# Router stage and first expert: kept memory re-laid, last ring place loaded sooner, biases moved, expert 0 gathered as columns

## The chip, the cores and the metric

One core of one Trainium2 chip runs the whole layer in one launch. The metric is the device time in microseconds (us); lower is better.

## What is computed

One decoder layer over 256 tokens of width 1024, in float32: a projection, a convolution group and a gated linear attention group, the output projection added to x (the sum is called x2 here), then a mixture of experts and a final norm. What matters here is the mixture:

```python
logits = (xf @ w_router + b_router).astype(jnp.float32)      # xf = RMSNorm(x2)
top_v, top_i = lax.top_k(logits, TOP_K)                      # 4 of 32
gates = jax.nn.softmax(top_v, axis=-1)
...
gu = xb @ w_gate_up[eid] + b_gate_up[eid]
gate = jnp.minimum(gu[:, :D_FF], SWIGLU_LIMIT)
up = jnp.clip(gu[:, D_FF:], -SWIGLU_LIMIT, SWIGLU_LIMIT)
glu = gate * jax.nn.sigmoid(gate * SWIGLU_ALPHA)
return ((up + 1.0) * glu) @ w_down[eid] + b_down[eid]
```

The weights of all 32 experts (12.6 MB each, 403 MB in all) have to come from memory.

## The kernel before

**Tiling.** The 256 tokens are two tiles (t = 0, 1) of 128. K = 1024 is eight blocks of 128 (k = 0 to 7). An item is one expert with up to 64 of its tokens (SLOTS); items 0 to 31 are the 32 experts in order, and further ones exist only for experts with more than 64 tokens.

**The ring.** Expert weights are loaded in chunks of 2 MB (4096 float32 on each of 128 partitions) into a ring of 12 places. An item has 6 chunks: 0 to 3 are gate and up, 4 and 5 are down, so the ring holds two items. The chunks are numbered g = 0, 1, 2, ...; SyncE (SP) issues the loads in the order of the list in its block, L496, each behind a wait: g = 1 to 11 wait for the mixer's buffers that lie in the same places, g = 12 and later wait until TensorE has used the chunk 12 before. g = 12 goes in four quarters (0.5 MB), g = 13 to 17 in halves (1 MB), since item 0's chunks free piece by piece (semaphores s_quarter, s_half, s_used). From item 6 on the loads go in pairs of 4 MB. g = 11, the last place, waits for s_lg 2, both tiles' logits: its place (10) holds the columns of x2 (h_t), the scaled router weights (wr_g) and the partial logits until then.

**The router stage.** TensorE (PE) runs the output projection, turns x2 into columns (L1606, transposes), and multiplies by the router weights (L1622 in parts for tile 0, L1612 for tile 1). ScalarE (ACT) copies columns and takes squares. VectorE (DVE) then makes, for each tile, logits (L1162), their eight largest (L1164), and the mask of the four chosen experts (L1165 to L1167, "chosen"). PE multiplies the mask by a triangle of ones to rank the tokens (L1663, L1678), DVE makes of it a selection matrix p_row for expert 0 (L1171, L1173), and PE gathers the rows of x2 by it (gather, L1634: the selection is the stationary operand, 512 columns of x2 stream past). ACT copies the gathered rows to x_row (L759), PE turns them (turn_first, L1700), DVE scales them into x_t (L1234), and the first product of item 0 (gate_up, L1750) can start. idle (L1562) is a matmul whose result is not used. Softmax gates are made beside this (L1199 to L1205, L1229), turned (L1705), and used from item 0's end on.

**An item.** gate_up over chunks 0 to 3, turn_gates (L1795) between chunks 0 and 1, turns of the result (L1789), down over chunks 4 and 5 (L1770), the gather and turn of the next item (L1634, L1692), and a scatter (L1814).

**The biases.** ACT issues the loads of b_gate_up (bias_t) and b_down (bdn, four pieces) early in the mixer, L666 to L669.

## Time and profile before

| | us |
|---|---|
| median of 3 runs | 1028.8 |
| lowest and highest | 1027.85, 1029.49 |
| profiled execution, device time | 1027.81 |
| its span on the core | 1026.0 |

Outside the span lie 1.8 us of the profiled execution. The granted TensorE clock of the span was 0.998 of full speed. The page's second part cuts the span into 40 equal slices of 25.65 us, and for each shows the engines' busy share in tenths, the share of the 16 DMA engines and the rate in GB/s. "Windows" below are the same for stretches that were asked for. The chain of waits is the work that ended last, followed back from the end. Times in the timeline are from the start of the span.

### The profile page before, as it was taken

To read this page: it belongs to the slowest core of one execution; us is meant where nothing else is said; L and a number is where in the kernel's file an instruction comes from. 1 tells how busy PE (TensorE), PEld (TensorE's weight loads), DVE (VectorE), ACT (ScalarE), POOL (GpSimd) and SP (SyncE) were. 2 spreads that over 40 slices of the span, in tenths; PEclk is the share of its full clock that TensorE was granted. 3 is DMA by queue.
4 is the path that set the end of the run, shared out by engine and by line. 5 is a ranking of instruction groups with operands and counts; after the bars stand their busy time and mean duration, and the time that the engine had idled before them with its cause. 6 is when DMAs were issued, how large, how long until landed. Compare 5 with 4: busy or idle time off the path is not lost.

```text
span 1026.0 us, 12540 instructions
## 1 busy us (share of the span) xinstructions
PE 1000.9 (98%) x5004; PEld 411.9 (40%) x5004; DVE 273.3 (27%) x673; ACT 149.6 (15%) x299; POOL 9.7 (1%) x27
## 2 busy tenths in 40 slices
PE   9999999999999999999999999999999999999996
PEld 7799733333333333333333333333333333333333
DVE  2878322222212222222222212222121212122122
ACT  2311211111111111111111111111111111111112
POOL 1010000000000000000000000000000000000000
PEclk9999999999999999999999999999999999999999
DMA  9996799999999999999999999999999999999995
GB/s 381 395 376 253 304 393 428 427 426 434 429 429 431 429 431 431 432 433 436 432 429 432 429 431 431 432 433 436 432 429 431 431 429 432 427 429 428 425 420 237
DMA packets 24716, 423.97 MB, mean 413 GB/s; under 512 B 3048, under 2 KB 3696, under 8 KB 6384
## 3 DMA queue, kind: packets, MB, share of 16 engines
q1 hardware_dynamic: 23328, 420.78, 96.5%
q10 hardware_dynamic: 1360, 2.79, 0.7%
q8 instruction: 21, 0.34, 0.1%
q14 instruction: 7, 0.06, 0.0%
HBM read 422.51 MB, written 1.05 MB: 413 GB/s over the span
## 4 chain that ended last, share of the span: by engine, by line
PE 80%; DMA 18%; issue 1%; DVE 0%; ACT 0%; SPq 0%; POOL 0%; ACTq 0%; PEldq 0%; DVEq 0%; POOLq 0%
PE bank L1750 34%; PE bank L1770 19%; DMA ring<-in_w_expert 18%; PE bank L1416 5%; PE y L1814 5%; PE bank L1634 5%; PE bank L1789 3%; PE bank L1692 1%; PE bank L1466 1%; PE bank L1408 1%; PE y L1567 1%; PE bank L1599 1%; PE bank L1795 1%; PE bank L1872 1%; PE y L1856 0%
## 5 line engine op out<-in xcount | busy, mean ns | idle before, releaser
L1750 PE MATMUL bank<-ring,x_t 128*64 128x512 f32 x1984 | 447.1, 597 | 0.0
L1770 PE MATMUL bank<-ring,act 128*64 128x512 f32 x992 | 230.8, 596 | 11.7 <-DMA ring<-in_w_expert 11.7
L1750 PEld LDWEIGHTS bank<-ring,x_t 128*64 128x64 f32 x1984 | 133.9, 136 | 261.9 <-issue 258.1
L1272 DVE TENSOR_TENSOR gu_b<-bank,bias_t 128x512 f32<-128x512 f32 x64 | 44.3, 692 | 326.6 <-PE bank L1789 326.5
L1770 PEld LDWEIGHTS bank<-ring,act 128*64 128x64 f32 x992 | 68.3, 137 | 142.9 <-issue 140.0
L773 ACT COPY gu_sb<-bank 128x512 f32<-128x512 f32 x64 | 37.5, 587 | 222.7 <-PE bank L1750 222.7
L1225 DVE TENSOR_TENSOR x_t<-bank,cols 128x512 f32<-128x512 f32 x30 | 20.8, 692 | 165.1 <-PE bank L1692 165.1
L1814 PE MATMUL y<-z,p_t 64*128 64x512 f32 x248 | 61.6, 615 | 0.0
L1634 PE MATMUL bank<-x_sb,p_row 128*64 128x512 f32 x256 | 60.6, 593 | 0.0
L1211 DVE TENSOR_SCALAR p_row<-slot,rank,rstd 128x64 f32<-128x64 f32 x62 | 16.7, 312 | 164.5 <-PE bank L1795 164.5
L777 ACT ACTIVATE act<-gu_b 128x256 f32<-128x256 f32 x62 | 25.9, 418 | 191.7 <-DVE gu_b L1278 191.7
L1789 PEld LDWEIGHTS bank<-ident,gu_sb 128*128 128x128 f32 x256 | 26.8, 140 | 50.7 <-issue 50.2
L1789 PE MATMUL bank<-ident,gu_sb 128*128 128x128 f32 x256 | 42.0, 286 | 0.1
L769 ACT COPY p_t<-bank 128x256 f32<-128x256 f32 x31 | 11.6, 373 | 189.2 <-PE bank L1795 189.2
L1634 PEld LDWEIGHTS bank<-x_sb,p_row 128*64 128x64 f32 x256 | 18.2, 137 | 35.6 <-issue 35.4
L781 ACT COPY z<-bank 128x512 f32<-128x512 f32 x31 | 18.2, 587 | 90.7 <-PE bank L1770 90.7
L1814 PEld LDWEIGHTS y<-z,p_t 64*128 64x128 f32 x248 | 21.3, 186 | 20.0 <-issue 14.6
L1288 DVE TENSOR_TENSOR act<-act,gu_b 128x256 f32<-128x256 f32 x62 | 26.4, 425 | 6.5
L1283 DVE SCALAR_TENSOR_TENSOR gu_b<-gu_b 128x256 f32<-128x256 f32 x64 | 27.2, 424 | 2.2
L765 ACT COPY x_row<-bank 128x512 f32<-128x512 f32 x31 | 18.2, 587 | 63.0 <-PE bank L1634 63.0
L1692 PEld LDWEIGHTS bank<-ident,x_row 128*128 128x128 f32 x124 | 13.0, 140 | 31.2 <-issue 31.2
L1692 PE MATMUL bank<-ident,x_row 128*128 128x128 f32 x124 | 19.5, 280 | 4.8 <-PE bank L1770 4.8
(264 smaller groups left out, 515.2 us busy)
## 6 DMA issues: line engine op xcount, KB each, us to landing
ring<-in_w_expert SPq DMA_DIRECT2D x66, 4096.0 KB, 34.3
ring<-in_w_expert SPq DMA_DIRECT2D x48, 2048.0 KB, 16.9
ring<-in_w_expert SPq DMA_DIRECT2D x18, 1024.0 KB, 10.1
ring<-in_w_in SPq DMA_DIRECT2D x4, 2048.0 KB, 27.4
ring<-in_w_out SPq DMA_DIRECT2D x2, 2048.0 KB, 28.9
ring<-in_w_in SPq DMA_DIRECT2D x2, 1024.0 KB, 13.3
ring<-in_w_expert SPq DMA_DIRECT2D x4, 512.0 KB, 4.3
ring<-in_w_down_last SPq DMA_DIRECT2D x4, 512.0 KB, 28.4
```

The source lines that it names most:

```text
L773: act_e.copy(gu_sb[:, h, :], bank[h][:, :]).then_inc(s_guk, 1)
L777: act_e.activation(act_of(it)[:, 4 * h:4 * h + 4, :], gu_b[:, 0, :, :], ACT.Sigmoid, scale=ALPHA).then_inc(s_sig, 1)
L1272: dve.tensor_tensor(gu_b[:, :, :, :], bank[2][:, :].rearrange("p (f a s) -> p a f s", a=2, f=4), bias_t[:, :, 4 * h:4 * h + 4, ds(e, 1)] . ...
L1283: dve.scalar_tensor_tensor(out=gu_b[:, 1, :, :], in0=gu_b[:, 1, :, :], scalar=1.0, in1=gu_b[:, 0, :, :], op0=ALU.add, op1=ALU.mult).then_i ...
L1288: dve.tensor_tensor(act_of(it)[:, 4 * h:4 * h + 4, :], act_of(it)[:, 4 * h:4 * h + 4, :], gu_b[:, 1, :, :], ALU.mult).then_inc(s_av, 1)
L1416: ins = mm(acc[:, m, :], w[:, k, m * P:(m + 1) * P], h[:, k, :], start=first and m == 0 and k == 0, stop=last and k == 3, skip_group_check ...
L1634: ins = mm(bank[3][a * SLOTS:(a + 1) * SLOTS, :], p_row[:, t, :], xs[:, t, a * HALF:(a + 1) * HALF], start=t == 0, stop=t == TT - 1)
L1692: ins = nc.tensor.transpose(bank[3][:, f * P:(f + 1) * P], x_row[:, f * P:(f + 1) * P], ident[:, :])
L1750: ins = mm(bank[h][a * SLOTS:(a + 1) * SLOTS, :], x_t_of(it)[:, k, :], w[:, kk, a, :], start=k == 0, stop=k == KT - 1)
L1770: ins = mm(bank[0][a * SLOTS:(a + 1) * SLOTS, :], act_of(it)[:, k, :], w[:, kk, a, :], start=k == 0, stop=k == KT - 1)
L1789: ins = nc.tensor.transpose(bank[2][:, f * P:(f + 1) * P], gu_sb[:, h, f * P:(f + 1) * P], ident[:, :])
L1814: mm(y_ps[t][nn][:, :], p_t_of(it)[r, t * P:(t + 1) * P], z[r, :], start=first, stop=False, skip_group_check=True).then_inc(s_y, 1)
```

## The change

1. **Kept memory.** The columns of x2 go to a tile of their own, h2 (8 KB a partition), in memory that later holds act, gu_b, p_t, bdn and gates_t. wr_g, parts_sb and ident4, and three new small tiles, go to where bias_t will be. Place 10 of the ring is thereby free after the sixth product of the output projection.
2. **The last place.** g = 11 is issued ahead of g = 9 and waits for that product instead of both logits.
3. **The biases** are now loaded by SP, ahead of g = 12: bdn (one piece, laid out on the host) behind s_lg 2, bias_t behind s_p0 2. ACT's five issues are gone.
4. **Expert 0 ranked alone.** For tile 1, DVE compares the logit of expert 0 with the fourth largest (first_c, one element a partition) instead of first making the whole mask; PE ranks that column alone; DVE makes p_row for tile 1 straight from PSUM. The mask, the full rank and the gates come later, beside item 0.
5. **Gathered as columns.** gather_first has 128 x 128 blocks of x2 as stationary operand and p_row (64 columns) streaming, so the columns x_t come out directly: no copy to x_row, no turn. It comes in three parts (k 0 to 1, 2 to 3, 4 to 7), each scaled by DVE by itself (keep_first). Tile 0's part is spread over the waits where idle stood; of tile 1, k 4 to 7, the full rank and the counts stand inside item 0, between its second and third k, and the turn of the gates between chunk 1's halves.

```diff
+        h2 = at("h2", [P, TT, KT, P], 16384)
+        wr_g, parts_sb, ident4, slot0, first_c, first_r = row((
...
+            def load_biases():
+                sp.wait_ge(s_lg, 2)
+                sp.dma_start(bdn[:, :], b_down).then_inc(s_bdn, 16)
+                sp.wait_ge(s_p0, 2)
+                sp.dma_start(bias_t[:, :, :, :], ...).then_inc(s_bias, 16)
+            for g in [0, 1, 2, 6, 7, 3, 4, 5, 8, 11, 9, 10] + list(range(12, len(LOAD_ORDER))):
...
                     elif g == 11:
-                        sp.wait_ge(s_lg, 2)
+                        sp.wait_ge(s_prod, PRODUCTS * len(BLOCKED) + 6)
...
+            def choose_first():
+                dve.tensor_tensor(first_c[:, :], lg[:, 1, 0:1], lmax[:, 1, TOP - 1:TOP], ALU.is_ge).then_inc(s_first, 1)
+                dve.wait_ge(s_first, 1)
+                dve.tensor_tensor(first_r[:, :], first_c[:, :], rstd[:, 1:2], ALU.mult).then_inc(s_first, 1)
...
+            mark_chosen(1)
+            keep_first(0, 0, 2, s_xt_a)
+            keep_chosen(1)
+            keep_first(1, 2, 4, s_xt_a)
...
+            def gather_first(t, ks):
+                for k in ks:
+                    i = 0 if k < 2 else 1 if k < 4 else 2
+                    k0 = (0, 2, 4)[i]
+                    ins = mm(bank[FIRST_BANK[i]][:, (k - k0) * SLOTS:(k - k0 + 1) * SLOTS], xs[:, t, k * P:(k + 1) * P], p_row[:, t, :],
...
+                if known == 0:
+                    gate_up(it, 0, range(0, 2))
+                    gather_first(1, range(4, KT))
+                    rank_second()
+                    gate_up(it, 0, range(2, 4))
+                    gate_up(it, 1, range(0, 2))
+                    turn_all_gates()
+                    turn_gates(it)
+                    gate_up(it, 1, range(2, 4))
```

On PE, from the end of the logits of tile 1 to the second chunk of item 0. Before, in program order (the last field is the operand's size and count; x_row are gathered rows, x_t the columns of the item):

```order
L1612 MATMUL y<-wr_g,g_h 128x32
L1674 MATMUL y<-chosen,ones 128x32 [waits first_p_row_ready]
L1634 MATMUL bank<-x_sb,p_row 64x512 x2
L1678 MATMUL y<-chosen,before 128x32 [waits chosen_ready]
L1680 MATMUL y<-ones,chosen 32x1 x2
...
L1700 MATMUL bank<-ident,x_row 128x128 [waits first_x_row_half_ready]
...
L1750 MATMUL bank<-ring_49,x_t 64x512 [waits slot11_loaded,first_x_t_half_ready]
L1750 MATMUL bank<-ring_49,x_t 64x512 x3
L1750 MATMUL bank<-ring_49,x_t 64x512 [waits x_t_ready]
```

After:

```order
L1652 MATMUL y<-wr_g,h_62 128x32
L1675 MATMUL bank<-p_row,x_sb 128x64 x5
L1727 MATMUL y<-chosen,ones 128x1
L1730 MATMUL y<-first_c,before 128x1 [waits second_tile_of_first_expert_chosen]
L1602 MATMUL bank<-before,ones 128x128
L1675 MATMUL bank<-p_row,x_sb 128x64 [waits first_p_row_ready]
L1675 MATMUL bank<-p_row,x_sb 128x64 x3
L1801 MATMUL bank<-ring_49,x_t 64x512 [waits slot11_loaded,first_x_t_columns_ready]
L1801 MATMUL bank<-ring_49,x_t 64x512 x3
L1675 MATMUL bank<-p_row,x_sb 128x64 x4
L1739 MATMUL y<-chosen,ones 128x32 [waits chosen_ready]
L1740 MATMUL y<-chosen,before 128x32
```

The full mask's wait (chosen_ready) and four of the gathering matmuls have moved behind the first two k of item 0, and the turn of x_row is gone.

On SP, the loads before item 0's first chunk is given back (ring_54 is two places, of them place 10; 128x4096 is a whole chunk). Before:

```order
L484 DMA ring_53<-in_w_expert 128x4096 [waits quadrant_ready,y_gla_ready]
L484 DMA ring_53<-in_w_expert 128x4096 [waits block_product_ready]
L484 DMA ring_54<-in_w_expert 128x2048 [waits out_projected] x2
L484 DMA ring_54<-in_w_expert 128x4096 [waits logits_ready]
L484 DMA ring_49<-in_w_expert 128x1024 [waits first_chunk_quarter_used] x3
```

After:

```order
L494 DMA ring_54<-in_w_expert 128x4096 [waits block_product_ready]
L494 DMA ring_53<-in_w_expert 128x4096 [waits block_product_ready]
L494 DMA ring_54<-in_w_expert 128x2048 [waits out_projected] x2
L508 DMA bdn<-in_b_down 128x512 [waits logits_ready]
L510 DMA bias_t<-in_b_gate_up 128x512 [waits first_p_row_ready]
L494 DMA ring_49<-in_w_expert 128x1024 [waits first_chunk_quarter_used] x3
```

The whole chunk of place 10 has moved ahead of three loads, and two bias loads stand between the ring's last filling and its first refill.

## Rows read from the trace of the kernel before

**Rows 1.** The page: rate in 40 slices; busy time and share of PE.

```profile
GB/s 381 395 376 253 304 393 428 427 426 434 429 429 431 429 431 431 432 433 436 432 429 432 429 431 431 432 433 436 432 429 431 431 429 432 427 429 428 425 420 237
PE 1000.9 (98%) x5004; PEld 411.9 (40%) x5004; DVE 273.3 (27%) x673; ACT 149.6 (15%) x299; POOL 9.7 (1%) x27
```

**Rows 2.** Windows: stretch and length, busy us (count) by engine, clock, DMA share, GB/s.

```profile
85.00:95.00 10.00, 10.00 (x83) 9.74 (x82) 9.22 (x18) 1.12 (x3) 0.00 (x0) 1.00 0.14 32
115.00:125.00 10.00, 9.71 (x72) 8.11 (x73) 4.27 (x20) 2.80 (x11) 0.00 (x0) 1.00 0.45 151
130.00:135.00 5.00, 5.00 (x26) 1.57 (x24) 2.16 (x10) 0.56 (x2) 0.00 (x0) 1.00 0.89 329
200.00:700.00 500.00, 497.12 (x2330) 170.51 (x2328) 108.67 (x288) 64.45 (x127) 0.00 (x0) 1.00 1.00 431
```

**Rows 3.** Waits of PE over the span: us in total, times, longest.

```profile
PE bank L1770 <- DMA ring<-in_w_expert: 11.7, 8, 1.8
```

**Rows 4.** The chain of waits in order of time: start, us, what.

```profile
129.76 3.58 PE bank L1750 x16
133.71 5.30 PE bank L1750 x24
156.92 3.58 PE bank L1750 x16
967.29 38.46 DMA ring<-in_w_expert
```

**Rows 5.** SP's load line in narrow windows: one issue's time, us to its landing.

```profile
L484 SPq DMA_DIRECT2D ring<-in_w_expert x1: 328/328/328, 124.7 to 124.7; - x1
DMA to landing us min/median/max: 7.5/7.5/7.5
...
L484 SPq DMA_DIRECT2D ring<-in_w_expert x1: 328/328/328, 130.8 to 130.8; - x1
DMA to landing us min/median/max: 3.5/3.5/3.5
...
L484 SPq DMA_DIRECT2D ring<-in_w_expert x1: 328/328/328, 132.5 to 132.5; - x1
DMA to landing us min/median/max: 4.8/4.8/4.8
...
L484 SPq DMA_DIRECT2D ring<-in_w_expert x1: 327/327/327, 137.3 to 137.3; - x1
DMA to landing us min/median/max: 7.3/7.3/7.3
```

**Rows 6.** Timeline of PE: start, us, line, operation, count.

```profile
124.08 0.63 PE L1612 MATMUL y<-wr_g,g_h 128*128 128x32 f32 x4
124.54 0.39 PE L1674 MATMUL y<-chosen,ones 128*128 128x32 f32 x2
126.07 0.41 PE L1678 MATMUL y<-chosen,before 128*128 128x32 f32 x2
127.11 1.08 PE L1634 MATMUL bank<-x_sb,p_row 128*64 128x512 f32 x4
129.69 1.51 PE L1750 MATMUL bank<-ring,x_t 128*64 128x512 f32 x6
```

**Rows 7.** Timeline of DVE and ACT in the same stretch.

```profile
121.46 0.15 DVE L1187 TENSOR_SCALAR rest<-rest 128x1 f32<-128x1 f32 x1
125.10 0.20 DVE L1164 MAX8 lmax<-lg 128x8 f32<-128x32 f32 x1
126.51 0.19 DVE L1171 SCALAR_TENSOR_TENSOR rank<-y,chosen 128x32 f32<-128x32 f32 x1 [0.50 <-PE y L1678]
126.74 0.31 DVE L1173 TENSOR_SCALAR p_row<-slot,rank,rstd 128x64 f32<-128x64 f32 x1
128.24 0.65 ACT L759 COPY x_row<-bank 128x256 f32<-128x256 f32 x2 [0.70 <-PE bank L1634]
129.14 0.43 DVE L1234 TENSOR_TENSOR x_t<-bank,cols 128x256 f32<-128x256 f32 x1 [0.30 <-PE bank L1700]
```

More of the change, by code:

```diff
@@ L297, in build @@
         s_late = sem("router_weights_loaded")
[L298 removed]
+        s_bias = sem("gate_up_biases_loaded")
+        s_bdn = sem("down_biases_loaded")
         s_gfin = sem("g_final_loaded")
@@ L665, in _ @@
             act_e.dma_start(br_bc[:, :], b_router.partition_broadcast(P)[:, 0, :]).then_inc(s_late, 16)
-            act_e.dma_start(bias_t[:, :, :, :], b_gate_up.rearrange("p (a f e) -> p a f e", a=2, f=F // P)).then_inc(s_bias, 16)
-            for i in range(SPLITS):
-                c = slice(i % 2 * HALF, (i % 2 + 1) * HALF)
-                act_e.dma_start(bdn[i * E:(i + 1) * E, :], b_down[0][:, c]).then_inc(s_bias, 16)
             def keep_v(n):
@@ L754, in _ @@
             act_e.activation(ex[:, :, :], ex[:, :, :], ACT.Exp).then_inc(s_le, 1)
-            for f in range(2):
-                act_e.wait_ge(s_xg, 1)
-                act_e.copy(x_row[:, f * 256:(f + 1) * 256], bank[3][:, f * 256:(f + 1) * 256]).then_inc((s_xr_a, s_xr)[f], 1)
             act_e.preload_act_table_set("sigmoid_and_others")
             def keep_gathered(it):
-                act_e.wait_ge(s_xg, it + 1)
+                act_e.wait_ge(s_xg, it)
                 act_e.copy(x_row[:, :], bank[3][:, :]).then_inc(s_xr, 1)
@@ L1181, in _ @@
             dve.wait_ge(s_lg, 1)
-            choose(0)
+            raw_to_logits(0)
+            mark_chosen(0)
+            keep_chosen(0)
             dve.wait_ge(s_const, 3)
-            rank_and_place(0)
+            link(rank(0))
+            dve.tensor_scalar(p_row[:, 0, :], slot1[:, 0:SLOTS], rank1[:, 0, 0:1], rstd[:, 0:1],
+                              ALU.is_equal, ALU.mult).then_inc(s_p0, 1)
             dve.wait_ge(s_ss, TT + 3)
@@ L1561, in idle @@
                 for _ in range(n):
-                    mm(bank[1][:, 0:P], ones[:, :], before[:, :], start=True, stop=True)
+                    mm(bank[0][:, 0:P], ones[:, :], before[:, :], start=True, stop=True)
             def multiply_rows(acc, y, w, first, last):
@@ L1667, in _, with rank_second @@
             logits(1, 4, 6)
+            pe.wait_ge(s_p0, 1)
+            gather_first(0, range(0, 1))
             pe.wait_ge(s_x2, 3)
             transpose_x(1, 6, 8)
[L1670 removed]
+            gather_first(0, range(1, 3))
             pe.wait_ge(s_trD, 1)
             logits(1, 6, 8)
[L1673 to L1681 removed]
+            gather_first(0, range(3, KT))
+            mm(bank[5][:, 2 * E:2 * E + 1], ones[:, :], chosen[:, 0, 0:1], start=True, stop=False)
+            pe.wait_ge(s_first, 1)
+            mm(bank[5][:, 2 * E:2 * E + 1], before[:, :], first_c[:, :], start=False, stop=True).then_inc(s_rk0, 1)
             idle(1)
             pe.wait_ge(s_p0, 2)
[L1684 to L1685 removed]
+            gather_first(1, range(0, 4))
             nb = BLOCKS - 1
+            def rank_second():
+                pe.wait_ge(s_cho, 2)
+                mm(bank[5][:, E:2 * E], ones[:, :], chosen[:, 0, :], start=True, stop=False)
+                mm(bank[5][:, E:2 * E], before[:, :], chosen[:, 1, :], start=False, stop=True).then_inc(s_rk, 1)
+                for t in range(TT):
+                    ins = mm(bank[7][0:E, 256:257], chosen[:, t, :], ones[:, 0:1], start=t == 0, stop=t == TT - 1)
+                ins.then_inc(s_cnt, 1)
             def turn_gathered(it):
[L1690 removed]
+                pe.wait_ge(s_xr, it)
                 for f in range(4):
@@ L1693, in turn_gathered, with turn_all_gates @@
                 ins.then_inc(s_xT, 1)
-            def turn_first():
-                for i in range(2):
-                    pe.wait_ge((s_xr_a, s_xr)[i], 1)
-                    for f in range(2 * i, 2 * i + 2):
-                        ins = nc.tensor.transpose(bank[(2, 4)[i]][:, f % 2 * P:(f % 2 + 1) * P], x_row[:, f * P:(f + 1) * P], ident[:, :])
-                    ins.then_inc((s_xT_a, s_xT)[i], 1)
-                    idle(1 - i)
+            def turn_all_gates():
                 pe.wait_ge(s_gtk, 2)
```

127 lines of the change are left out of this document (70 added, 57 removed).

## Prediction

> **What bounds the kernel now.** First the page's rates and busy shares [rows 1]: PE is busy 98% of the span, yet from the seventh slice on the rate stands at 425 to 436 GB/s and does not move. The windows say the same: 431 GB/s at a DMA share of 1.00 over the 500 us from 200 to 700 [rows 2]. So two engines look full at once, and the question is which would finish first alone. The chain of waits answers it. Item 0 begins at 129.76 and item 1 at 156.92 [rows 4]: 27.2 us of PE work for an item. Its 12.6 MB at 431 GB/s take 29.2 us. PE therefore runs ahead by 2 us an item, gives ring places back sooner than they can be filled, and late in the kernel stands still for weights, eight times and 11.7 us in all [rows 3]; the last long stretch of the chain is 38.46 us of expert loads [rows 4]. From item 0 to the end the kernel is a queue of loads that never runs dry. A microsecond of PE work in the items is worth nothing; the time can fall only if this queue starts sooner.
>
> When does it start? The ring holds twelve chunks, and the thirteenth (g = 12) needs a quarter of item 0's first chunk given back. Its first quarter is issued at 130.8 and lands 3.5 us later [rows 5], against PE's start of item 0 at 129.69 [rows 6]: 1.12 us from start to issue. The last place, g = 11, is issued at 124.7 and lands after 7.5 us, at 132.2 [rows 5]. So before, the two conditions meet at nearly the same moment: the loads have just filled the ring when the first quarter comes free. Ahead of that the loads idle, at 32 GB/s from 85 to 95 and 151 GB/s from 115 to 125 [rows 2]. Moving one of the two conditions alone gains nothing, and this change moves both.
>
> **The last place early.** One chunk of 2 MB takes 2.1/431 = 4.9 us. Issued behind the sixth product of the output projection instead of at 124.7, it runs in the 151 GB/s stretch, where two thirds of the rate, over 6 us, are unused [rows 2]. It delays g = 9 and 10 by at most its 4.9 us, and those are first used in item 1, 27 us on. The ring is then full about 127. Worth by itself: nothing, since the first quarter is not there yet.
>
> **The start of item 0.** I walk the path from the logits of tile 1, whose products and maxima I leave where they are: the two parts of tile 0's gathering put before them take the place of idle or of a wait. The maxima are ready at 125.10 + 0.20 = 125.30 [rows 7].
> - DVE: first_c is a one-column operation, 0.15 us [rows 7]: 125.48. Before, three operations stood here, to 126.07 on PE.
> - PE is not free then. The four instructions of the last two k take (124.54 - 124.08)/4 = 0.115 us each [rows 6]: the price of a full 128 x 128 stationary operand. Five k of tile 0's gathering are ten such, 1.12 us: 125.66. The product with ones, two more: 125.88. So PE, not DVE, is late by 0.4 us, and this is new.
> - The rank of one column: from the start of such a pair to DVE's use, 126.51 - 126.07 = 0.44 us [rows 6, 7]: 126.32. p_row 0.31, hand-over 0.06: PE gathers at 126.69 (before 127.11 [rows 6]).
> - Two k of tile 1: 0.44 + 0.22 = 0.66: 127.35. The scaling of 128 columns: 0.43 us for 256 [rows 7] makes about 0.30. Hand-over 0.12: item 0 starts at 127.77.
> - Gone are the four wide gathering instructions (1.08 us), the copy to x_row (0.65 for its two halves) and the first turn.
>
> That is **1.9 us earlier** (129.69 - 127.77), and so is the first quarter: issue at 128.9.
>
> **What is put into item 0.** Between its second and third k now stand four k of gathering (8 x 0.11 = 0.9), two rank products (0.45) and the counts (0.2 to 0.3): about 1.65 us. The third quarter is given back at 132.5 - 1.9 + 1.65 = 132.25, only 0.25 us sooner than before [rows 5]. The first chunk is done 0.3 us sooner; the gates' turn (0.2) between chunk 1's halves uses this up, and from the end of chunk 1 (137.3 for its last issue [rows 5]) PE is where it was. The waits in the inserted part are met: chosen is made by 127.9, and x_t for k 2 and 3 by 128.3, against a use after 131. DVE now waits for the gates' turn near 135 and must place item 1's rows after it (0.5 + 0.6 us), done by 137.3, while its next work arrives at 139.6: covered by 2 us. If that cover went, PE would turn later, but PE has the lead.
>
> **What the loads make of it.** Quarters 0 and 1 land 1.9 us sooner, at 132.4 and 133.6. Quarter 2, issued at 132.25, lands at best behind them, 133.6 + 1.2 = 134.9, at worst as a cold one, 132.25 + 3.5 = 135.8. Before it was 132.5 + 4.8 = 137.3 [rows 5]. The gain at this point is thus between 1.5 and 2.4 us. At the second half of chunk 1, issued at 137.3 in both, a queue without slips would be at 141.9 against 137.3 + 7.3 = 144.6 [rows 5]. Before, the shallow queue lost some 1 us there (four quarters and two halves are 9.8 us of data from the first landing's start, and 144.6 is later). A queue that is shallow for longer can lose it again. I take the cold bound, **1.5 us**: nearest to what a first load after a pause showed.
>
> By the Trainium skill ("DMA: Bandwidth & Descriptors", Anatomy of one DMA) a transfer costs about 2.0 us fixed plus its bytes at 436 GB/s; that makes 3.2 us for a quarter where the row shows 3.5, and with the fixed part paid once more at quarter 2 the gain would be 1.8 us instead of 1.5. The row is used.
>
> **The biases.** 0.5 MB is 1.2 us of loading. It leaves the mixer, where PE is busy throughout and the expert chunks wait for PE, so nothing is gained. It returns at 124.8 and 126.7 into the pause before 129.8 that the early last place leaves: free there. Had the queue no pause, it would cost up to 1.2 us. SP issues each in about 0.4 us and is free again before the first quarter. bias_t is awaited on DVE before item 1's rows, near 136; it lands by about 130. ACT's reordered copies come before its waits for PE.
>
> **Sum.** 1027.81 - 1.5 = 1026.3 for an execution like the profiled one, which ran 1.0 us under the median; against the median 1028.8, **1027.3 us**.
>
> **Rivals.**
> - *All of it and the slips too.* The longer lead of the first quarters lets the queue absorb the third: 134.9 at quarter 2, and the slip behind chunk 1 goes: 2.1 to 2.7 us, time 1026.4. For it: the last place no longer overlaps the first quarter. Against it: that quarter 2 comes only 0.25 us sooner.
> - *Nothing carried over.* What counts is not the first quarter but the third and the rest of item 0, which PE gives back as before. If some later issue, say that of item 1's first chunk, already arrives just in time, the lead ends there: gain 0.2 us, time 1028.6. For it: PE's total work to the end of chunk 1 is the same. Against it: the landing delay grows to 7.3 us by 137.3 [rows 5], so the queue has depth from there.
> - *Slower.* Gathering as columns costs PE more: the rows show 0.115 us an instruction with 32 columns streaming, not 64 with this stationary operand from x2. If each takes the 0.28 us that a single one lasts instead, the 22 instructions and four others up to the third quarter add 26 x 0.165 = 4.3 us: quarter 2 is issued at 136.6, lands at 140.1, 2.8 us later than before; time 1031.6. It turns slower when quarter 2 is issued after 133.8 (137.3 - 3.5).
> - *The change doesn't do what it says:* a load order in which the last place still waits. The order of SP's loads excludes it.
>
> **Chances.** Forecast (gain 0.8 to 2.0) 0.47; all and the slips 0.27; nothing carried 0.20; slower 0.06. A measurement of this kernel can tell some 0.2%, 2.06 us, from no change. The first rival lies just beyond it, and the forecast's upper end just below: faster 0.30. The forecast and the second rival are within it: same 0.64. Slower by so much needs the third: 0.06. The range 1025.9 to 1029.0 takes in the forecast, most of both neighbours and half a microsecond by which medians of three differ; it leaves out the slower case.
>
> **What would show it.** Item 0's first product near 127.8; PE's wait for first_c short or none, with DVE waiting for the rank; the last place issued near 103; the first quarter's issue near 128.9 and the third's near 132.3; the rate near zero just before 129.8, then unbroken from 134 on; item 1 beginning at 156.9 as before; the last load of the chain 1.5 us sooner. The forecast is wrong if the first product comes later than 128.5, if the column products take over 0.15 us each, or if the rate falls below 400 GB/s between 145 and 200.

## The result, and the profile after

| | before | after |
|---|---|---|
| median, us (12 runs each, same chip) | 1028.39 | 1030.09 |
| lowest and highest, us | 1027.23, 1029.49 | 1027.9, 1035.7 |
| profiled execution, device time and span, us | 1027.81, 1026.0 | 1031.04, 1029.3 |
| mean granted clock of that span | 0.998 | 0.994 |

The ratio is 1.002, with a 95% interval of 1.0011 to 1.003: the change makes the kernel a little slower, and far more scattered. The forecast was 1027.3 us, its range ended at 1029.0.

The page looks as before: the rate and PE's share beside [rows 1].

```profile
GB/s 379 424 318 255 371 307 422 427 427 434 428 429 431 432 436 430 429 429 433 430 437 430 429 430 433 430 436 429 429 430 433 432 434 429 425 427 427 427 420 235
PE 1004.0 (98%) x5018; PEld 415.2 (40%) x5018; DVE 273.5 (27%) x676; ACT 148.5 (14%) x297; POOL 9.8 (1%) x28
```

The windows of the kernel after (as [rows 2]: stretch, length, busy us and count of PE, PEld, DVE, ACT, POOL, clock, DMA share, GB/s) show what the page hides.

```profile
115.00:125.00 10.00, 9.88 (x76) 8.42 (x74) 4.14 (x20) 3.71 (x14) 0.00 (x0) 1.00 0.81 323
121.00:127.00 6.00, 5.88 (x46) 5.33 (x45) 3.32 (x16) 1.66 (x6) 0.00 (x0) 0.99 0.69 254
127.00:133.00 6.00, 5.83 (x19) 2.86 (x18) 1.89 (x11) 0.89 (x1) 0.00 (x0) 0.50 0.39 113
200.00:700.00 500.00, 497.11 (x2330) 170.61 (x2327) 106.73 (x283) 64.43 (x127) 0.00 (x0) 1.00 1.00 431
```

From 127 to 133 us TensorE's granted clock is 0.50: the lower of its two levels, 1.2 GHz, at the very place where item 0 begins. The same window of before stands at the upper level, 2.4 GHz; ahead of it PE was busy for 5.58 of 6.00 us.

```profile
121.00:127.00 6.00, 5.58 (x38) 4.12 (x37) 3.55 (x19) 1.01 (x4) 0.00 (x0) 1.00 0.62 223
127.00:133.00 6.00, 6.00 (x33) 2.64 (x32) 3.28 (x14) 2.19 (x4) 0.00 (x0) 1.00 0.90 349
```

The stretch from 115 to 125 us has its 323 GB/s (151 in [rows 2]), so the gap is filled: the last place's own load has landed by 116.8, and the loads that it pushed back run there. The timelines of PE and DVE show the path (as [rows 6, 7]).

```profile
125.24 0.25 DVE L1173 SCALAR_TENSOR_TENSOR lg<-y,rstd,br_bc 128x32 f32<-128x32 f32 x1
125.75 0.16 DVE L1191 TENSOR_TENSOR first_c<-lg,lmax 128x1 f32<-128x1 f32 x1
126.31 0.36 PE L1730 MATMUL y<-first_c,before 128*128 128x1 f32 x2
126.81 0.32 DVE L1199 TENSOR_SCALAR p_row<-slot,y,first_r 128x64 f32<-128x64 f32 x1 [0.56 <-PE y L1730]
127.18 1.97 PE L1675 MATMUL bank<-p_row,x_sb 128*128 128x64 f32 x8 [0.17 <-DVE p_row L1199]
128.41 0.29 DVE L1236 TENSOR_TENSOR x_t<-bank,cols 128x128 f32<-128x128 f32 x1 [0.91 <-PE bank L1675]
129.08 3.68 PE L1801 MATMUL bank<-ring,x_t 128*64 128x512 f32 x8
134.82 2.37 PE L1801 MATMUL bank<-ring,x_t 128*64 128x512 f32 x10
```

Executions differ by up to 2 us in the first stage, ahead of all this, so I measure everything from the start of the logits of tile 1 on DVE. That is 125.24 here and 124.81 before:

```profile
124.81 0.25 DVE L1162 SCALAR_TENSOR_TENSOR lg<-y,rstd,br_bc 128x32 f32<-128x32 f32 x1
```

Up to p_row (1.57 us behind the logits) it goes as forecast. Then the gathering of four k takes 1.97 us for eight instructions, 0.25 each, and the first eight products of item 0 take 3.68 us where sixteen should. The chain of waits has the rest:

```profile
132.76 1.49 PE bank L1675 x8
134.89 3.58 PE bank L1801 x16
966.37 42.06 DMA ring<-in_w_expert
```

SP's load line in narrow windows (as [rows 5]), for the last place, the first and the third quarter: the issues are at 103.8, 131.1 and 135.9. Before, the quarters stood at 130.8 and 132.5.

```profile
L494 SPq DMA_DIRECT2D ring<-in_w_expert x1: 327/327/327, 103.8 to 103.8; - x1
DMA to landing us min/median/max: 13.0/13.0/13.0
...
L494 SPq DMA_DIRECT2D ring<-in_w_expert x1: 328/328/328, 131.1 to 131.1; - x1
DMA to landing us min/median/max: 3.5/3.5/3.5
...
L494 SPq DMA_DIRECT2D ring<-in_w_expert x1: 327/327/327, 135.9 to 135.9; - x1
DMA to landing us min/median/max: 3.9/3.9/3.9
```

One more row differs, at the very end. The last store of the output, in before (L573) and in after (L591), and the queue line of the window that starts with the latter:

```profile
L573 SPq DMA_DIRECT2D out<-y_out x1: 399/399/399, 1023.0 to 1023.0; - x1
DMA to landing us min/median/max: 2.7/2.7/2.7
```

```profile
L591 SPq DMA_DIRECT2D out<-y_out x1: 408/408/408, 1025.7 to 1025.7; - x1
DMA to landing us min/median/max: 3.2/3.2/3.2
...
q14 instruction: 1, 0.01, 0.5%
```

The store takes 0.5 us longer, and one packet of queue 14, which carries instructions, lies in its window; before has none there.

So the 3.3 us between the two spans (1029.3 - 1026.0) split into three, all worked out from rows. The logits came 0.43 later. The chain's last expert load landed at 966.37 + 42.06 = 1008.43, which is 883.2 behind the logits; before it was 967.29 + 38.46 = 1005.75 [rows 4], 880.9 behind: 2.25 us. And from there to the end it takes 20.9 instead of 20.25: 0.6 us.

The fallen clock is not in every execution, as far as the mean over the whole span tells. In the five runs with a mean clock of 0.999 the time is 1027.9 to 1029.2; in the seven with 0.997 or less it is 1029.86 to 1035.7. Even the good ones (middle 1028.84) are no faster than before.

### The profile page after: what moved, and what is told of

It is laid out like the page before. It is cut to its first block, busy times and chain, and to the rows that moved or that the text cites. A ratio compares the mean times of both kernels' runs of the same rounds, so it can differ in the third digit from the quotient of the medians.

```text
span 1029.3 us, 12548 instructions
## 1 busy us (share of the span) xinstructions
PE 1004.0 (98%) x5018; PEld 415.2 (40%) x5018; DVE 273.5 (27%) x676; ACT 148.5 (14%) x297; POOL 9.8 (1%) x28
## 4 chain that ended last, share of the span: by engine, by line
PE 79%; DMA 19%; SPq 1%; issue 0%; ACT 0%; DVE 0%; ACTq 0%; another core or an unknown queue 0%; POOL 0%; PEldq 0%; DVEq 0%; POOLq 0%
PE bank L1801 33%; PE bank L1821 18%; DMA ring<-in_w_expert 18%; PE bank L1456 5%; PE y L1865 4%; PE bank L1684 4%; PE bank L1840 3%; PE bank L1749 1%; PE bank L1448 1%; PE y L1607 1%; PE bank L1506 1%; PE bank L1639 1%; PE bank L1846 1%; SPq L568 1%; PE bank L1933 1%; DMA ring<-in_w_qk 1%
## 5 line engine op out<-in xcount | busy, mean ns | idle before, releaser
L1801 PEld LDWEIGHTS bank<-ring,x_t 128*64 128x64 f32 x1984 | 134.3, 137 | 261.8 <-issue 258.3
L1684 PE MATMUL bank<-x_sb,p_row 128*64 128x512 f32 x248 | 58.5, 592 | 0.0
```

The source lines that it names most:

```text
L1684: ins = mm(bank[3][a * SLOTS:(a + 1) * SLOTS, :], p_row[:, t, :], xs[:, t, a * HALF:(a + 1) * HALF], start=t == 0, stop=t == TT - 1)
L1801: ins = mm(bank[h][a * SLOTS:(a + 1) * SLOTS, :], x_t_of(it)[:, k, :], w[:, kk, a, :], start=k == 0, stop=k == KT - 1)
```

## Experiments

Every kernel was timed in 11 or 12 runs beside the kernel before. Its medians in the four batches are 1028.68 (e1 to e4), 1028.6 (e5 to e8), 1028.38 (e9 to e13) and 1028.53 (e14 to e16). "Behind the logits" counts from the start of DVE's logits of tile 1. The last three columns come from one profiled execution each. The intervals reach about 0.9 us to either side.

| kernel | median | ratio, 95% interval | item 1 begins, behind the logits | last load landed, behind the logits | from there to the end |
|---|---|---|---|---|---|
| before | 1028.38 to 1028.68 | | 32.0 | 880.9 | 20.25 |
| after | 1030.09 | 1.0011 to 1.003 | 35.3 | 883.2 | 20.9 |
| e1_twice_streamed | 1028.17 | 0.9986 to 1.0004 | 32.3 | 879.6 | 20.8 |
| e2_wide_fill | 1028.75 | 0.9993 to 1.0011 | 32.8 | 880.0 | 20.9 |
| e3_memory_loads_only | 1028.58 | 0.9990 to 1.0008 | 32.0 | 880.15 | 20.3 |
| e4_before_no_idle | 1030.46 | 1.0007 to 1.0025 | 32.0 | 880.8 | 21.9 |
| e5_twice_and_after_chunk0 | 1028.0 | 0.9986 to 1.0004 | 32.4 | 880.0 | 20.9 |
| e6_moved_after_chunk0 | 1029.01 | 0.9997 to 1.0015 | 33.9 | 881.5 | 20.9 |
| e7_twice_late_place | 1028.71 | 0.9992 to 1.0010 | 32.3 | 879.8 | 20.9 |
| e8_before_work_in_chunk0 | 1029.8 | 1.0004 to 1.0022 | 33.95 | 881.7 | 20.3 |
| e9_no_idle_same_length | 1030.86 | 1.0010 to 1.0033 | 34.8 | 883.7 | 20.3 |
| e10_next_chunk_in_halves | 1028.55 | 0.9991 to 1.0008 | 32.4 | 879.9 | 20.8 |
| e11_halves_and_later_rank | 1029.24 | 0.9999 to 1.0017 | 33.3 | 880.9 | 20.9 |
| e13_before_work_after_next | 1028.43 | 0.9991 to 1.0009 | 32.05 | 881.8 | 20.3 |
| e14_longer_vector | 1028.37 | 0.9992 to 1.0010 | 32.4 | 880.0 | 20.8 |
| e15_longer_scalar | 1027.87 | 0.9986 to 1.0004 | 32.4 | 879.8 | 20.3 |
| e16_longer_sync | 1028.48 | 0.9991 to 1.0009 | 32.4 | 879.8 | 20.9 |

### The clock: e1, e2, e4, e6

**e1_twice_streamed.** The changed kernel, but every matmul that gathers for expert 0 streams the 64 columns of p_row twice, and DVE reads the first 64 of each result:

```diff
-                dve.tensor_tensor(x_t[:, k0:k1, :], bank[FIRST_BANK[i]][:, 0:n * SLOTS].rearrange("p (k s) -> p k s", k=n),
+                dve.tensor_tensor(x_t[:, k0:k1, :], bank[FIRST_BANK[i]][:, 0:n * P].rearrange("p (k s) -> p k s", k=n)[:, :, 0:SLOTS],
...
-                    ins = mm(bank[FIRST_BANK[i]][:, (k - k0) * SLOTS:(k - k0 + 1) * SLOTS], xs[:, t, k * P:(k + 1) * P], p_row[:, t, :],
+                    twice_p = p_row[:, t, :].rearrange("p (a s) -> p a s", a=1).broadcast_to([P, 2, SLOTS])
+                    ins = mm(bank[FIRST_BANK[i]][:, (k - k0) * P:(k - k0 + 1) * P].rearrange("p (a s) -> p a s", a=2), xs[:, t, k * P:(k + 1) * P], twice_p,
```

> The changed kernel, but each column-gathering matmul streams the 64 columns of the selection twice (128 columns, the second half is not used). An instruction with a full stationary operand takes 0.115 us either way, so the path is not longer. Theory C (clock): the changed kernel loses because the granted clock falls to half near 127 us, after a stretch in which TensorE streamed few columns; with twice the columns the clock stays at 1.00, item 0 starts near 127.8 us and the median falls under that of the changed kernel by 1 to 3 us. Theory Q (queue): the clock is a bystander, the loss comes from the work put into item 0; then the median stays at 1030 even if the clock holds. If the clock still falls, twice is not enough and neither is decided.

1.9 us less than the changed kernel (0.5 below its own before, where the changed kernel lies 1.7 above; the intervals of the two don't meet), and the scatter is gone (1027.47 to 1029.16). The same window, and in PE's timeline the gathering and item 0's first product:

```profile
127.00:133.00 6.00, 5.81 (x41) 3.70 (x42) 3.01 (x15) 1.48 (x2) 0.00 (x0) 1.00 0.70 221
...
127.79 1.16 PE L1676 MATMUL bank<-p_row,x_sb 128*128 128x128 f32 x8 [0.18 <-DVE p_row L1199]
128.95 1.94 PE L1802 MATMUL bank<-ring,x_t 128*64 128x512 f32 x8
```

The clock stays up: no run of this kernel has a mean under 0.997. (The mean alone is a coarse sign. This very execution has 0.997, and none of its windows shows a fall.) The product starts 128.95 - 125.84 = 3.11 us behind the logits, against 3.84 in the changed kernel and 4.88 before. Twice the columns at half the price: the eight instructions take 1.16 us, not 1.97. That settles the main cause of the loss, the clock.

**e2_wide_fill.** e1, and in tile 0's gathering an unused matmul of 512 columns takes the place of k 1 and 2, which move behind PE's last products of the logits:

```diff
-            gather_first(0, range(1, 3))
+            fill()                        # one matmul of 512 columns
...
-            gather_first(0, range(3, KT))
+            gather_first(0, range(1, KT))
```

> As the one with twice-streamed columns, and in the wait for the last columns of x2 a matmul with 512 columns whose result is unused; tile 0's gathering of k 1 and 2 comes after the logits instead. It puts item 0 back by about 0.5 us if nothing else changes. Theory C: the clock holds at 1.00 from 123 to 134 us, and the median is below that of the changed kernel by 1 to 3 us in spite of the longer path. Theory Q: no better than the changed kernel, worse by 0.5 us.

The clock stays up here too, and the moved gathering costs what it weighs: item 1 begins 0.4 us later than in e1. Nothing is gained over e1.

**e4_before_no_idle.** The kernel before without its idle matmuls:

```diff
             def idle(n):
-                for _ in range(n):
-                    mm(bank[1][:, 0:P], ones[:, :], before[:, :], start=True, stop=True)
+                pass
```

> The kernel before without its seven unused matmuls of 128 columns between 123 and 129 us; nothing waits for them. Theory C: they keep the granted clock up; without them it falls to half in some executions and the time spreads and rises by 0.5 to 3 us. Rival: gathering rows, with 512 streamed columns, is enough by itself; then the clock stays 1.00 and the time is that of before within 0.3 us.

It is 1.8 us slower, but the profiled execution has a clock of 1.00 in every window from 121 to 134, and its loads end as in before. The loss stands in the last column of the table; the section on the end of the kernel takes it up.

**e6_moved_after_chunk0.** The changed kernel with the inserted work behind item 0's first chunk, not inside it:

```diff
-                    gate_up(it, 0, range(0, 2))
+                    gate_up(it, 0, range(4))
                     gather_first(1, range(4, KT))
                     rank_second()
-                    gate_up(it, 0, range(2, 4))
```

> The changed kernel with only that move: the inserted work behind all four k of chunk 0; the row is streamed once, 64 columns, as in the changed kernel. Theory (granted clock): the narrow column gathers still stand ahead of item 0, the granted clock still falls from about 127 to 133 us in at least part of the executions, and the median lies at 1029 to 1030, at least 1 us above e5. Rival (the order of the work inside item 0 is what costs, not the clock): the time falls to e5's, near 1027.5.

With 64 columns the clock falls again. Its mean is under 0.997 in five of eleven runs, with 1029.01 to 1030.56; the other six lie at 1027.89 to 1030.26. Only the number of columns tells this kernel from e5 below, and the two were timed together: e5 has no such run, and its median is 1028.0 beside 1029.01. In the profiled execution the granted clock is 0.83 from 127 to 128 and 0.50 from there to 131, and 1.00 again from 132 on.

```profile
127.86 5.24 PE L1801 MATMUL bank<-ring,x_t 128*64 128x512 f32 x16
133.02 1.10 PE L1675 MATMUL bank<-p_row,x_sb 128*128 128x64 f32 x8
```

The sixteen products take 5.24 us, where e5 has 3.65, and item 1 begins 1.5 us later behind the logits than in e5. The eight gathering instructions behind them, at the upper clock, take 1.10 us with 64 columns. So the narrow instructions are not dear by themselves, as the "slower" rival had it; the fallen clock is what costs. Nor does the order inside item 0 make the clock fall. Whether that order adds to the price in the changed kernel, whose median is 1.1 us above e6's, is not settled, for the intervals overlap.

### Where the lead ends: e3, e5, e7, e8, e10, e11, e13

**e3_memory_loads_only.** Parts 1 to 3 of the change without the new ranking and gathering:

```diff
+        h2 = at("h2", [P, TT, KT, P], 16384)
...
-            for g in [0, 1, 2, 6, 7, 3, 4, 5] + list(range(8, len(LOAD_ORDER))):
+            for g in [0, 1, 2, 6, 7, 3, 4, 5, 8, 11, 9, 10] + list(range(12, len(LOAD_ORDER))):
...
+                if g == RING:
+                    load_biases()
...
-                        sp.wait_ge(s_lg, 2)
+                        sp.wait_ge(s_prod, PRODUCTS * len(BLOCKED) + 6)
```

> The kernel before with the memory and the loads of the change (x2's columns, router weights and partial logits in kept memory, the last ring place behind the sixth output product, biases by SP), but with the ranking and the gathering of rows as before. The first quarter of the ring's refill is then released as before, near 130.8 us. Theory: within 0.3 us of the kernel before, since item 0's start sets the refill; the clock stays at 1.00. Rival: the early place or the late biases cost by themselves, then it is 1 us or more slower than before and the ranking is not to blame.

Nothing that can be told (1028.58 beside 1028.68), as the prediction said of the last place alone.

**e5_twice_and_after_chunk0.** e1 and e6 in one.

```diff
-                    gate_up(it, 0, range(0, 2))
+                    gate_up(it, 0, range(4))
                     gather_first(1, range(4, KT))
                     rank_second()
-                    gate_up(it, 0, range(2, 4))
```

> As e1 (p_row streamed twice, clock expected to stay at full), and the work inserted between k 1 and k 2 of item 0's first chunk (gathering of five k's rest, second expert's rank) stands behind all four k of chunk 0. Theory: the third quarter of the ring place decides how much of the lead is carried, because it comes back only after the inserted 1.65 us; so its issue comes 1.65 us sooner than in e1 and the time is about 1 us under e1's 1028.2, at 1027.2. Rival: later returns, or the slips of the shallow queue, decide; then the same as e1, 1028.2 within 0.3. Second rival: the inserted work now delays chunk 1 and the lead ends there: also e1's time.

The third quarter is issued at 132.3, 5.95 behind the logits, where e1 has it at 133.6, 7.8 behind; e1's then lands as a cold one, after 3.5 us. The 1.8 us are worth nothing that can be told: 1028.0 beside 1028.17, and the loads end no sooner. But e5's third quarter lands only after 5.2 us, so the two land 11.15 and 11.26 us behind the logits, alike. The sooner issue is lost in the queue; what a sooner landing would bring, this run doesn't show.

**e7_twice_late_place.** e1 with the old load order and the old wait of the last place:

```diff
-            for g in [0, 1, 2, 6, 7, 3, 4, 5, 8, 11, 9, 10] + list(range(12, len(LOAD_ORDER))):
+            for g in [0, 1, 2, 6, 7, 3, 4, 5] + list(range(8, len(LOAD_ORDER))):
...
-                        sp.wait_ge(s_prod, PRODUCTS * len(BLOCKED) + 6)
+                        sp.wait_ge(s_lg, 2)
```

> e1 with the ring's last place loaded as before: order g = 8, 9, 10, 11, the last waiting for the logits of tile 1. Theory of the prediction (both conditions are needed): the last place lands behind or beside the first quarter, the lead of 1.8 us is used up by its 4.9 us of data, and the time goes back to the kernel before, 1028.7. Rival (the last place early is worth nothing even then): e1's time, 1028.2.

1028.71 against e1's 1028.17 has the sign that was expected, but the intervals overlap, and in the profiled executions the last loads land within 0.2 us of each other. Whether the early place is worth anything is not settled; the medians put it at half a microsecond, and the intervals allow nothing as well as more than twice that.

**e8_before_work_in_chunk0 and e13_before_work_after_next.** The kernel before with seven unused matmuls (14 instructions, 1.76 us in e8's chain), once inside item 0's first chunk, once behind item 1's second:

```diff
-                gate_up(it, 0, range(4))
+                if known == 0:
+                    gate_up(it, 0, range(0, 2))
+                    idle(7)
+                    gate_up(it, 0, range(2, 4))
+                else:
+                    gate_up(it, 0, range(4))
```

```diff
                 gate_up(it, 1, range(4))
+                if known == 1:
+                    idle(7)
```

> The kernel before with 1.5 us of unused matmuls (14 instructions of full stationary operands) between k 1 and k 2 of item 0's first chunk; nothing is left out. Theory (the third quarter's return decides, a delay of it delays every later load): 0.8 to 1.5 us slower than before, 1029.5 to 1030.2. Rival (the queue's depth or PE's lead covers it): same as before, 1028.7 within 0.3.

> The kernel before with the same 1.5 us of unused matmuls as in e8, but behind item 1's second chunk instead of inside item 0's first. Theory: the last return that still binds the loads is that of item 1's first chunk (g = 18); what TensorE loses behind it costs nothing: the same as before, 1028.6 within 0.3, where e8 cost 1.2. Rival: later returns of item 1 bind as well, and it costs 1.2 to 1.5 as in e8: 1029.8.

In item 0 it costs 1.2 us; behind item 1's second chunk 0.05. So PE's work inside item 0 is on the path, though PE "has the lead". That the same work a chunk into item 1 costs nothing is what the medians say, but it is not shown firmly: e13's interval reaches 0.9 us to either side, the two kernels were not timed together, and in e13's profiled execution, one of its slower ones (1029.82), the loads end 0.9 us later than before's.

**e10_next_chunk_in_halves.** The first load into item 1's place had looked like the point: g = 18, the first that is issued whole. In before and in e5:

```profile
L484 SPq DMA_DIRECT2D ring<-in_w_expert x1: 327/327/327, 160.5 to 160.5; - x1
DMA to landing us min/median/max: 9.1/9.1/9.1
```

```profile
L494 SPq DMA_DIRECT2D ring<-in_w_expert x1: 328/328/328, 162.5 to 162.5; - x1
DMA to landing us min/median/max: 8.5/8.5/8.5
```

Behind the logits these are 35.7 and 36.15: e5 issues it 0.45 us later than before did, its first product 1.8 us sooner notwithstanding. e10 is e5 with this load cut in two:

```diff
-IN_PARTS = {10: 2, 12: 4, 13: 2, 14: 2, 15: 2, 16: 2, 17: 2}
+IN_PARTS = {10: 2, 12: 4, 13: 2, 14: 2, 15: 2, 16: 2, 17: 2, 18: 2}
-                    elif isinstance(it, int) and it == 0 and kk == 1:
+                    elif isinstance(it, int) and (it == 0 or it == 1 and j == 0) and kk == 1:
                         ins.then_inc(s_half, 1)
```

> e5 with the load of item 2's first chunk (g = 18, into the place of item 1's first) cut into halves, the first of them issued when item 1 has used its first two k. Theory: in e5 the lead was kept to lg + 38.5 us and lost in one step at g = 18, a whole chunk of 2 MB issued at 36.1 and landed 8.2 us later; in halves its first part is issued about 1.8 us sooner, so nothing is lost there and the time is 0.5 to 0.9 us below e5: 1027.2 to 1027.6. Rival: the next whole chunk (g = 19) loses it instead, or the stretched packets do: the same as e5, 1028.0 to 1028.3.

The rival came true: 1028.55, the same as e5 within what can be told. One load is not the place.

**e11_halves_and_later_rank.** e10 with the second tile's rank behind the first half of chunk 1 and the gates' turns behind its second:

```diff
-                    rank_second()
                     gate_up(it, 1, range(0, 2))
+                    rank_second()
+                    gate_up(it, 1, range(2, 4))
                     turn_all_gates()
                     turn_gates(it)
-                    gate_up(it, 1, range(2, 4))
```

> e10 with the second tile's full rank and the counts moved on, behind the first half of item 0's second chunk, and both turns of the gates behind its second half: the first half of that chunk comes back about 0.7 us sooner than in e10. Theory (after the first chunk every return of item 0 arrives just in time, so TensorE's work ahead of it is worth its own length): 0.3 to 0.7 us below e10, 1026.7 to 1027.2. Rival: the returns of chunk 2, which stay where they were, decide: the same as e10.

Not faster but slower, by 0.7 us against e10, timed together with it. PE's timeline shows why; the last field is its idle time ahead and what ended it.

```profile
132.39 1.16 PE L1676 MATMUL bank<-p_row,x_sb 128*128 128x128 f32 x8
134.15 1.94 PE L1802 MATMUL bank<-ring,x_t 128*64 128x512 f32 x8 [0.61 <-DVE x_t L1236]
```

The rank had hidden DVE's scaling of the columns. Without it PE stands still for 0.61 us there. Item 1 begins 33.3 us behind the logits instead of 32.4, and the last load lands 1.0 later.

**Read together.** When PE reaches item 1 and when the last load lands go together in the table, though not in all of it. These four rows are the start of item 1 in before, e5, e8 and after; behind the logits they are 32.0, 32.4, 33.95 and 35.3.

```profile
156.85 3.65 PE L1750 MATMUL bank<-ring,x_t 128*64 128x512 f32 x16
```

```profile
158.76 3.65 PE L1802 MATMUL bank<-ring,x_t 128*64 128x512 f32 x16
```

```profile
159.71 3.65 PE L1750 MATMUL bank<-ring,x_t 128*64 128x512 f32 x16
```

```profile
160.49 3.65 PE L1801 MATMUL bank<-ring,x_t 128*64 128x512 f32 x16
```

Among the kernels with the new gathering, from 32.3 to 35.3 us (e1, e5, e10, e11, e6, after) the last load lands at 879.6, 880.0, 879.9, 880.9, 881.5 and 883.2: about a microsecond for each microsecond by which PE comes late to item 1. The landing less the arrival is 847.3 to 847.9 us in all eleven kernels with the new gathering. The first product of item 0 doesn't order them: it stands 3.11 us behind the logits in e1, e5 and e11 alike, and in e6, with its last load at 881.5, even at 3.06.

Without the new gathering it is otherwise. There the same difference is 848.9 in before, 848.1 in e3, 848.8 in e4, 847.8 in e8, 848.9 in e9 and 849.8 in e13: the loads end later than PE's arrival at item 1 alone would have it. That fits a queue which in before still waits for its start, as the prediction said, and in the new kernels for PE's arrival at item 1. It is an argument from one execution each, and e9 and e13 don't fit it.

### The end of the kernel: e9, e14, e15, e16

e4's last store, and the queue line of its window:

```profile
L573 SPq DMA_DIRECT2D out<-y_out x1: 393/393/393, 1023.6 to 1023.6; - x1
DMA to landing us min/median/max: 4.2/4.2/4.2
```

```profile
q8 instruction: 1, 0.02, 1.4%
```

4.2 us instead of 2.7, beside one packet of queue 8, of 16 KB. These 1.5 us are most of e4's 1.8.

**e9_no_idle_same_length.** e4 with its program made as long as before's again, by six more matmuls in the warm-up at the start:

```diff
-            for _ in range(8):
+            for _ in range(14):
                 mm(bank[7][:, 0:P], ones[:, :], ones[:, :], start=True, stop=True)
```

> The kernel without the idle matmuls (e4) with six matmuls more in the warm-up at the program's start, whose results are not used: TensorE's program is as long again as that of the kernel before. Theory: e4's 1.8 us were not the missing idle matmuls but an instruction fetch of queue 8 (one packet of 16 KB) that fell into the last store of the output, which landed 4.2 us after its issue, not 2.7; with the length restored the last store lands after 2.7 us, no instruction packet lies in its window, and the time is 1028.6 to 1029. Rival: the idle matmuls themselves were worth it; then the time stays at 1030.4.

The last store lands after 2.7 us again, with no instruction packet in its window. But now the clock falls: the mean is 0.997 or less in eight of twelve runs, all of 1030.28 or more, and the other four are at 1027.88 to 1029.27. In the profiled one it falls at 129 us:

```profile
129.00:136.00 7.00, 6.31 (x18) 2.44 (x20) 3.39 (x14) 2.19 (x4) 0.00 (x0) 0.51 0.63 264
```

So e4's loss was the fetch: without it, the four runs of e9 whose clock held are as fast as before. That the idle matmuls hold the clock is not shown. The mean is under 0.997 in seven of twelve runs of e9, but in one of eleven of e4, which lacks the same idle matmuls, and in two of 128 of before. e9 differs from before in two things, and six more warm-up matmuls without the other were not run. Why e4 kept its clock and e9 didn't, with the same instructions in this stage, stays open.

**e14_longer_vector, e15_longer_scalar, e16_longer_sync.** e5 with ten waits more, all long met, in the program of one engine:

```diff
+            for _ in range(10):
+                act_e.wait_ge(s_const, 1)     # e15; e14: dve, e16: sp
```

> e5 with ten waits more in VectorE's program, between the items that are written out and its loop; each is long met, and all that it changes is where the instructions behind it lie. In e5 and every kernel of the changed family the last store of the output lands 3.2 us after its issue, with one instruction packet of queue 14 (8 KB) in its window; in the kernel before 2.7, with none. Theory A: the packet fetches VectorE's instructions; ten instructions more move it out of the window, the store lands after 2.7 us, and the time is 0.5 us below e5's 1028.0 (less than the measurement can settle, so the landing decides). Rival: it belongs to another engine, and the landing stays at 3.2.

> e5 with ten met waits more in ScalarE's program ahead of its loop. Theory B: the packet in the last store's window fetches ScalarE's instructions; then here, and not in e14, the landing goes to 2.7 us and the packet leaves the window. Rival: it stays at 3.2.

> e5 with ten met waits more in SyncE's program behind its last load and ahead of the stores. Theory C: the packet fetches SyncE's own instructions; then here alone the landing goes to 2.7 us. Rival: it stays at 3.2.

Last stores of e14 and e15:

```profile
DMA to landing us min/median/max: 3.2/3.2/3.2
...
q14 instruction: 1, 0.01, 0.3%
```

```profile
L591 SPq DMA_DIRECT2D out<-y_out x1: 395/395/395, 1022.9 to 1022.9; - x1
DMA to landing us min/median/max: 2.7/2.7/2.7
```

Of the three programs, only ScalarE's moves it: 2.7 us and no packet in e15, 3.2 and one packet in e14 and e16. The ten other kernels with the new gathering, e14 and e16 among them, all have 3.2. So the packet fetches ScalarE's instructions. Why the change put it into the last store is argued, not shown: its ScalarE program is shorter (297 instructions in the page against 299, and five DMA issues fewer). The missing DMA issues alone don't do it, for e3 lacks them too, has 299 instructions, and its last store lands after 2.5 us without a packet. e15 has the lowest median here, 1027.87 us beside 1028.53, and is the only kernel whose eleven runs all lie under 1028.6; its interval still holds 1.

## Why the prediction was wrong

**The queue of loads as the bound: right.** The rate and the waits late in the kernel are as before (the page's rows above). PE's waits for weights, as [rows 3]:

```profile
PE bank L1821 <- DMA ring<-in_w_expert: 11.1, 8, 1.8
```

**The last place and the biases: right, as far as can be told.** Issued at 103.8, free, and worth nothing alone (e3).

**The start of item 0: right with the clock kept.** Forecast was 127.77 - 124.81 = 2.96 us behind the logits; e1 and e5 have 3.11, and p_row and the rank came when they should. The inserted work was put at 1.65 us; e1's chain runs from 130.89 to 132.56, 1.67.

**The step that failed first: that PE's durations stay what they were.** "0.115 us each" for full stationary operands was read at the upper clock and carried into a stretch whose work the change had made narrow: 64 columns an instruction, where 512 streamed before. In the profiled execution the clock fell, each column product then took 0.25 us, item 0's first quarter came back 1.8 us later than was forecast against the logits (5.9 for 4.1), its third 3.2 later (10.7 for 7.45), and item 1 began 3.2 us later than before. By the mean clock this happened in up to seven of twelve executions. The prediction has no word on the clock, as a term or as a rival. Two of its signs of being wrong came true, the first product later than 128.5 (129.08) and the column products over 0.15 us (0.25); the third did not, for the rate from 145 to 200 is 420 GB/s. Its "slower" rival had the place and even the test right (the third quarter issued after 133.8: it was 135.9, or 135.5 with the later logits taken off), with a price for the wrong reason: it laid the price on the width of the instructions, and e6 shows them cheap at the upper clock. I gave it 0.06. PE's busy time could not have warned: it was 5.88 of 6.00 us from 121 to 127, ahead of the fall. By the Trainium skill ("TensorE: Matmul & The Clock Gate", Why this matters for your kernels) what has to be avoided is gaps in which PE idles; here the trace differs, for there was none worth the name, the engine counted as busy, and what kept the clock was twice the columns in the same instructions.

**The step that failed second: "the gain at this point is thus between 1.5 and 2.4 us", carried to the end.** The prediction itself had written that from the end of chunk 1 PE is where it was, and that item 1 begins as before. That was most of the answer. The kernels with the clock kept (e1, e5, e7, e10, e14 to e16) start item 0 1.77 us sooner, and yet reach item 1 at 32.3 to 32.4 us against 32.0. Their medians, e15's aside, lie from 0.6 us under (e5) to 0.2 over (e10) that of the kernel before; over e1, e5, e7, e10, e14 and e16 the mean is 0.2 under. They all pay the 0.5 us longer last store of the next paragraph, so some 0.7 us of the 1.5 reach the last load. That is an estimate; e15, which doesn't pay it, is 0.66 under, with an interval from 1.4 under to 0.4 over. The profiled executions of e1, e5, e10, e14 and e16 say 0.9 to 1.3 against before's, but only 0.15 to 0.5 against e3's, which starts item 0 as before does. What takes the rest, as far as these runs tell, is PE's arrival at item 1 (e11, e6, e8), which the inserted work had put back to where it was. The mistake was to take the growing landing delay (7.3 us at 137.3) for depth.

The rival "nothing carried over", at 1028.6 and a chance of 0.20, comes near these kernels' times, 1027.9 to 1028.7. In part that is luck: the longer store, which no rival has, hides what was carried.

**Not in the sum: the end of the program.** 0.5 to 0.6 us from a fetch of instructions in the last store (e15).

Together, in the profiled execution: +3.2 us on PE up to item 1, of which 2.25 reach the last load, and +0.6 at the end, and 0.4 from the first stage, where executions of all kernels differ as much.

In the medians, as an estimate: 1028.39 for the kernel before (0.4 under the 1028.8 that the forecast started from), less 0.7 of lead carried, plus 0.5 for the store, is 1028.2. The remaining 1.9 us to 1030.09 are put down to the clock; in e6, whose clock stayed down for a shorter time in the profiled execution, it costs 1.0 beside e5.

**Slips in the working.** Ten instructions at 0.115 us are 1.15, not 1.12. From the first quarter's data (134.3 - 1.2 = 133.1) 9.8 us lead to 142.9, so before lost 1.7 us by 144.6, not "some 1"; the same sum 1.9 us sooner gives 141.0, not 141.9. None of this changes the forecast's 1.5. The section of the Trainium skill that the prediction names gives its 2.0 us and 436 GB/s for transfers issued by GpSimd; these loads are issued by SyncE, and their row, 3.5 us, was what the forecast used.

## What to carry to other kernels

When a change makes TensorE's matmuls narrower just ahead of a critical stretch, count the clock as a rival and look at the granted clock of that stretch in several executions; streaming unused columns may be cheaper than the clock. When two engines run in balance, a head start of one is worth only what is left of it at the last point where the other still waits for it: look for that point by putting work in front of and behind it, with enough runs to tell the two apart. And a few instructions more or less can move a fetch into the last store: compare the landing of the last store before any story about the middle.

## What the runs showed of the hardware that I had not expected

- TensorE's clock fell to 0.50 after a stretch in which PE was busy for 5.88 of 6.00 us with narrow float32 matmuls, and stayed up in before after 5.58 of 6.00 us. It differs between executions of one kernel: the mean is under 0.997 in 3 of 12, 5 of 11 and 7 of 12 runs of after, e6 and e9, in 2 of 128 of before (at 1030.98 and 1031.09 us), and in none of the 99 runs of the nine kernels that stream 128 columns. A mean of 0.997 tells little: four more runs of after have it, all slow, but so do 5 of the 128 and 11 of the 99.
- At the upper clock eight gathering instructions took 1.16 us with 128 columns (e1) and 1.10 with 64 (e6); with 64 columns at the lower clock 1.97 us.
- Packets that carry instructions share the DMA engines with data. With one of 8 KB in its window the last store took 0.5 us longer (e14 beside e15), with one of 16 KB 1.5 us (e4 beside before and e9). By the Trainium skill ("Advanced Engine Details and Errata", ISA Cache) the instruction cache has lines of 16 KB; the trace has packets of that size on queue 8 alone, and of 8 KB on queue 14.
